# Steps of the next projection put into the last units of two attentions

## What is computed

```
# block 1: 8 heads; o_a is the recurrent branch, o_b the latent attention ("mla")
y_a = o_a @ w_out_dn
o_b = mla_attention(...)
y_b = o_b @ w_out_mla
mix = sigmoid(gate_dn) * y_a + sigmoid(gate_mla) * y_b
x = x + gate1 * (mix @ w_o)
...
# block 2: 8 heads; y_b is the sparse attention ("dsa")
y_b = dsa_attention(q, k, v, q_idx, k_idx, w_idx)
merged = g_a * (y_a @ w_o_rwkv) + g_b * (y_b @ w_o_att)
h = h + merged @ w_out
```

## Time and profile before

| | |
|---|---|
| median of 3 runs | 2029.47 us (2026.11 to 2029.76) |
| the profiled execution | 2029.86 us |
| its span in the profile | 2028.1 us |
| PE busy | 1972.6 us, 97% of the span |
| POOL, DVE, ACT busy | 992.2, 918.6 and 823.1 us |
| share of PE in the chain that ended last | 88% |

### The profile page before, as it was taken

The page is one execution under the profiler, slowest core; times in us unless marked ns, Lnnn a source line. Parts: engine busy times, 40 slices in busy tenths (PEclk is TensorE's granted clock), DMA queues, the critical chain, the costliest instruction groups (busy, mean ns, idle before and its releaser), DMA issues.

```text
span 2028.1 us, 26209 instructions
## 1 busy us (share of the span) xinstructions
PE 1972.6 (97%) x10110; PEld 1605.9 (79%) x10110; DVE 918.6 (45%) x1502; ACT 823.1 (41%) x1098; POOL 992.2 (49%) x767
## 2 busy tenths in 40 slices
PE   6999999999999999999999999999999999999997
PEld 3787987867778878888888678977877788888886
DVE  2678648967331324222101886459954521112101
ACT  4567234346561333232222755254336542222321
POOL 3737634645215555565655572043542356555662
PEclk9999999999999999999999999999999999999999
DMA  7312025531112322222223220033221222222222
GB/s 290 105 63 84 22 86 232 207 110 63 38 46 104 131 98 84 104 85 103 104 104 135 104 84 22 2 103 108 97 83 63 109 99 95 92 104 94 97 101 83
DMA packets 30827, 199.59 MB, mean 98 GB/s; under 512 B 5488, under 2 KB 7664, under 8 KB 9712
## 3 DMA queue, kind: packets, MB, share of 16 engines
q1 hardware_dynamic: 30704, 197.92, 27.0%
HBM read 188.99 MB, written 4.19 MB: 95 GB/s over the span
## 4 chain that ended last, share of the span: by engine, by line
PE 88%; DVE 6%; ACT 3%; DMA 1%; issue 1%; POOL 0%; SPq 0%; DVEq 0%; ACTq 0%; POOLq 0%
PE ps L451 23%; PE ps L452 23%; PE ps L453 23%; PE ps L527 2%; PE ps L469 1%; PE ps L470 1%; DMA ar<-ada_dram 1%; PE ps L903 1%; PE ps L557 1%; PE ps L492 1%; PE ps L890 1%; PE ps L667 1%; PE ps L1226 1%; DVE ps L2039 1%; PE ps L1234 1%
## 5 line engine op out<-in xcount | busy, mean ns | idle before, releaser
L2669 POOL TENSOR_TENSOR WL<-raw,WH 128x512 fp32r<-128x512 f32 x588 | 782.6, 1331 | 852.1 <-ACT WH L1383 809.7
L451 PE MATMUL ps<-hH,WH 128*128 128x512 f32 x1560 | 619.6, 397 | 2.8 <-ACT ar L1447 1.6
L453 PE MATMUL ps<-hH,WL 128*128 128x512 f32 x1560 | 608.3, 390 | 0.0
L452 PE MATMUL ps<-arR,WH 128*128 128x512 f32 x1352 | 526.0, 389 | 0.0
L1383 ACT CAST WH<-raw 128x2048 fp32r<-128x2048 f32 x147 | 280.9, 1911 | 472.8 <-DMA raw<-panels_dram 471.7
L451 PEld LDWEIGHTS ps<-hH,WH 128*128 128x128 f32 x1560 | 293.5, 188 | 74.8 <-issue 13.7
L453 PEld LDWEIGHTS ps<-hH,WL 128*128 128x128 f32 x1560 | 293.4, 188 | 62.2
L452 PE MATMUL ps<-xL,WH 128*128 128x512 f32 x792 | 309.6, 391 | 0.0
L452 PEld LDWEIGHTS ps<-arR,WH 128*128 128x128 f32 x1352 | 253.8, 188 | 52.9 <-issue 0.5
L451 PE MATMUL ps<-arR,WH 128*128 128x512 f32 x584 | 227.9, 390 | 0.0
L453 PE MATMUL ps<-arR,WL 128*128 128x512 f32 x584 | 227.2, 389 | 0.0
(11 more groups left out here) (408 smaller groups left out, 2401.1 us busy)
## 6 DMA issues: line engine op xcount, KB each, us to landing
raw<-panels_dram SPq DMA_DIRECT2D x145, 1024.0 KB, 4.8
ar<-ada_dram SPq DMA_DIRECT2D x12, 2048.0 KB, 11.2
xT<-xT_dram SPq DMA_DIRECT2D x2, 2048.0 KB, 8.7
out_dram<-xT SPq DMA_DIRECT2D x8, 512.0 KB, 2.8
ar<-ar SPq DMA_DIRECT2D x12, 256.0 KB, 7.1
xT<-out_dram SPq DMA_DIRECT2D x1, 2048.0 KB, 9.2
wide<-wide_dram SPq DMA_DIRECT2D x1, 1024.0 KB, 4.8
ar<-ar SPq DMA_DIRECT2D x8, 128.0 KB, 3.9
```

Of the source, the lines that this page charges most:

```text
L451: mm(out, lhs[0], rhs[0], start=first, stop=False)
L452: mm(out, lhs[0], rhs[1], start=False, stop=False)
L453: return mm(out, lhs[1], rhs[0], start=False, stop=final)
L2669: ins = tt(WL[:, n % SLOTS, c], raw[:, n % SLOTS, c], WH[:, n % SLOTS, c].bitcast(F32), ALU.subtract)
```

## The change

Three things. `DENSE_STEPS` becomes a table over all 18 values of u: u = 1 takes 5 steps where it took 2, u = 15 takes 3 where it took 4, u = 16 and 17 take 2 each. The eight gate jobs are used up by the first step of u = 15, and the generator goes on with `begun`: k = 0 to 2 of job 0 and then of job 1 of the next projection (`y_dn0` in block 1, `ya` in block 2), six steps, in the banks 6 and 7. After the attention `rest` adds the steps that are left, five a job in `y_dn0` and one a job in `ya`, and `project` goes on with job 2. In block 1 the two turns of the bank counter are added by hand; in block 2 all later banks move round by two.

```diff
-DENSE_STEPS = (8, 2, 2, 4)
+DENSE_STEPS = (8, 5, 2, 4, 8, 2, 2, 4, 8, 2, 2, 4, 8, 2, 2, 3, 2, 2)
@@
+            def begun(stage, src, ready, kt, kn=3):
+
+                w = panel(stage, 0, PANEL // kt)
+                for i in range(2):
+                    begin(stage, i, DENSE_BANKS)
+                    for k in range(kn):
+                        pe.wait_ge(*ready(k))
+                        product(pst(stage, i), [x[:, k, i * P:(i + 1) * P] for x in w], src(k), k == 0, False)
+                        yield
+
+            def rest(stage, src, ready, kt, kn=3):
+
+                w = panel(stage, 0, PANEL // kt)
+                for i in range(2):
+                    for k in range(kn, kt):
+                        pe.wait_ge(*ready(k))
+                        ins = product(pst(stage, i), [x[:, k, i * P:(i + 1) * P] for x in w], src(k), False, k == kt - 1)
+                    end(ins, (stage, i))
+                    done_with(stage, 0)
@@
-                    for _ in range(DENSE_STEPS[u % NT]):
+                    for _ in range(DENSE_STEPS[u]):
                         next(dense, None)
@@
+                o_dn, o_dn_low = parts_in(O_DN_HIGH, range(V0, V0 + 8)), lambda k: part_ready("low", "o_dn", k)
                 attention("mla", UNITS, score, value, (12, 13, 14, 11), (15, 48),
-                          chain(woven("gate_dn0", h_mix, 2, 2), woven("gate_mla0", h_mix, 4), woven("gate_dn1", h_mix, 2)))
+                          chain(woven("gate_dn0", h_mix, 2, 2), woven("gate_mla0", h_mix, 4), woven("gate_dn1", h_mix, 2),
+                                begun("y_dn0", o_dn, o_dn_low, KD)))
+                rest("y_dn0", o_dn, o_dn_low, KD)
+                if counting:
+                    jobs.turns[ALL_BANKS] += 2
+                project("y_dn0", o_dn, 2, i0=2)
@@
-                attention("dsa", UNITS, score, value, (30, 31, 32, 29), (33, 34), woven("gate_b", h_mix, 8))
-                project("ya", parts_in(OA_HIGH, range(OA, OA + 4)), 8, lambda k: part_ready("low", "o_dsa", k), kt=4, per=4)
+                o_dsa, o_dsa_low = parts_in(OA_HIGH, range(OA, OA + 4)), lambda k: part_ready("low", "o_dsa", k)
+                attention("dsa", UNITS, score, value, (30, 31, 32, 29), (33, 34), chain(woven("gate_b", h_mix, 8), begun("ya", o_dsa, o_dsa_low, 4)))
+                rest("ya", o_dsa, o_dsa_low, 4)
+                project("ya", o_dsa, 6, kt=4, per=4, i0=2)
```

More of the change, by code:

```diff
@@ L912, in block_1 @@
                         project("gate_dn1", h_mix, 2, i0=2)
-                    project(f"y_dn{fb}", parts_in(O_DN_HIGH, range(V0, V0 + 8)), 4, lambda k: part_ready("low", "o_dn", k))
+                        project("y_dn1", o_dn, 4)
                     if fb:
```

## The result

The changed kernel takes 2037.22 us (median of five executions, 2034.02 to 2040.30) against 2029.47 before: ratio 1.0042, 95% interval 1.0032 to 1.0053. It is slower by 7.75 us, 5.3 us over the forecast and outside the range. A second set of five gave 2037.48, ratio 1.0047 (1.0034 to 1.0060). The profiled execution of the first set is its slowest: 2040.3 us, span 2038.5, mean granted clock 0.990.

What follows compares the result with a forecast made beforehand. PE, busy 97% of the span, was taken as the bound. Block 1 +2.4, block 2 -1.9 and one clock fall +1.5 gave +2.0 us on 2029.86: 2031.9 us, range 2027.0 to 2035.2.

Steps and rivals of the forecast that it cites:

- u = 1: Both attentions: three more steps close the waits at u = 2; PE 1.21 us behind in block 1, 1.2 ahead in block 2.
- Bank 7 in block 1: End of block 1's attention: new PE wait of 1.6 us until ACT copies the gate job; `rest` begins at 590.5 us.
- The panel of y_mla0: Block 1, after the attention: panel ready 2.9 us later, PE waits 3.6 us, `y_mla0` starts 2.4 us later than before.
- Rival (b): The panel of y_mla0 is no bound, only bank waits are left and no clock fall: 2026.8 us, chance 0.15.
- Rival (a): The steps fill all six idle times and the slow stretch, nothing replaces them: saves 8.8 us, 2021.1 us, chance 0.05.
- Block 2's tail: End of block 2's attention: PE waits 2.0 us for bank 7 and 1.9 for k = 3; block 2 sums to -1.9 us.
- The clock: Granted clock: one fall behind the wait before `y_mla0`, +1.5 us; shorter new waits may go either way.
- I take one fall, 1.5 us: Block 1: a single clock fall behind the 3.6 us wait before `y_mla0`, costing 1.5 us.
- rival (c): The clock falls at the shorter waits too, one in each tail beside the panel's: +5.0 us, 2034.9 us, chance 0.25.
- the credit of 1.6 us: Block 2, u = 2: the old stretch at low clock goes, gaining 1.6 us, counted inside block 2's -1.9.
- The base: The sum was added to the profiled execution's own 2029.86 us; the median of three runs was 2029.47.
- the forecast without its clock terms: The whole kernel's +2.0 us without the 1.5 us fall and the 1.6 us gain in block 2: +2.1 us.

Runs made afterwards that it cites:

- changed_again: The changed kernel itself run and profiled once more, with no further edit: median 2037.48 us, ratio 1.0047; the profiled execution was its fastest, span 2030.5 us.
- filled_three: Changed kernel with added matmuls of unused result in the waits for y_mla0's panel, bank 7 in block 2 and k = 3 of ya: 2032.13 us, ratio 1.0023.
- u1_spread: Kernel before with five steps at u = 1, the three more taken from u = 3, 7 and 11, nothing begun early: 2029.46 us, ratio 0.9999.
- before_filled: Kernel before with 13 added matmuls in the 3.26 us wait at 757.00 us, before the stage up: 2029.84 us, ratio 1.0003.

## Why the prediction was wrong

**u = 1: right.** Both waits went. In block 2 PE gained 1.3 us there, 1.2 forecast.

**Bank 7 in block 1: right.** 1.48 us of idle released by the gate copy (1.6), the transposes of unit 15 at 584.81 (584.8), `rest` at 590.38 (590.5).

**The panel of y_mla0: right.** ACT's cast moved from 601.42 to 604.25, by 2.8 us (2.9), PE idle for 3.11 us (3.6), `y_mla0` at 611.70 where the earlier trace rows has 609.44: +2.3 (+2.4). Rival (b) falls. Rival (a) falls with the bank waits.

**Block 2's tail: right in its waits.** 2.00 us for the bank (2.0), 1.96 for k = 3 (1.9). Not foreseen, 0.59 us for the low part of k = 2. In the execution without falls (`changed_again`) block 2 stood at -2.0 (-1.9), because the profile of before has its fall at u = 2.

**The clock: this step failed, in two terms.** The first is "I take one fall, 1.5 us". The price was right (1.65); the number was not. In the profiled execution three of the four long new waits had one behind them; over all executions they cost 4 to 5 us (`filled_three`), so two to three in the mean, not one, and about two by the count of the profiles. I had the rows for it: a fall behind 1.63 us and behind 3.26, none behind 1.34 and 1.43 nor behind 2.55. From two for and three against, waits of 2.0 us had about even chances each, one more fall in the sum; I gave them to rival (c) only. The second term is the credit of 1.6 us for the fall of the earlier trace rows, a chance event in one execution, taken as if it were in every one. Together the two terms came to -0.1 us; the mean clock fell from 0.9949 to 0.9917, which is 4.8 to 6.4 us at the two prices of the table. Rival (c), with three falls, gave 2034.9, the nearest; it kept the credit too, and its count was right by luck: it put one fall into each tail, where the profile has none in block 1's and two in block 2's. Without the credit it gives 2034.9 + 1.6 = 2036.5 on the profiled execution's base, 0.7 under what was measured.

**The base.** I compared two single executions where one execution of either kernel can be 5 us off for falls alone. Mean clock and time move together in every kernel: 1.5 us per 0.001 over all, 1.0 to 2.0 in the single ones.

**What stays open.** The falls in the recurrent part of block 2, 4.4 us of the profiled execution. No run shows whether the change makes them more frequent. With the three waits filled the mean is still 2.4 us over the forecast without its clock terms and the mean clock 0.0011 under that of before; where those falls stand is not shown.

## What to carry to other kernels

Price a wait of a saturated engine twice: its idle time, and the lower clock behind it. Here three new waits of 1.8 to 3.1 us cost 4 to 5 us more in the mean, 1.65 for each fall; a fourth of 1.48 us drew none in six profiles. So moving work into a gap pays only if nothing opens a gap elsewhere: look who frees the bank and who prepares the next weights, and move those first (two such lines turned +8 us into -4 by medians, into -2.4 by means). And never book a clock fall from one profile as a gain: look at the mean clock over all executions.

## What the runs showed of the hardware

- The same program ran from 2034.0 to 2040.3 us in five executions; the granted clock (0.994 to 0.990) orders them almost exactly.
- A fall can come behind 1.96 to 2.10 us of idle (1591.65 and 1600.30 above; 1580.15 in `u1_spread`) or fail to come behind 1.77 and 1.96 (1586.65 and 1593.86 in `changed_again`). The Trainium skill, "TensorE: Matmul & The Clock Gate", section "HAM oscillation — how this bites in real kernels", puts the falls down to idle gaps between bursts; for three waits `filled_three` agrees, for the one at 757 `before_filled` shows no gain from closing it.
- A fall can be long where the idle times are short: 10.2 us at 0.50 from 1321.7, at waits of 1.03 and 0.83 us that the kernel before has too, at 1.00.
- Matmuls whose results nobody uses, put into three waits, made the changed kernel 4 to 5 us faster, and its mean clock rose from 0.9917 to 0.9938.
